# Gated linear attention's three input projections as high and low parts, with modulation strips 2 to 5 taken chunk by chunk

## What is computed

```python
mod = c_act @ mod_w[l] + mod_b[l]
sh1, sc1, g1, sh2, sc2, g2 = jnp.split(mod, 6, axis=-1)
h = modulate(x, norm_g[l, 0], sh1, sc1)
# gla_mixer(h, ...)
proj = h @ w_in
q, k, v, og, gl = jnp.split(proj, [H * dk, 2 * H * dk, 2 * H * dk + H * dv, 2 * H * dk + 2 * H * dv], axis=-1)
log_a = jax.nn.log_sigmoid((gl @ w_g2 + b_g2).astype(jnp.float32)) / GLA_GATE_TAU
...
o = rmsnorm(o, norm_g) * jax.nn.silu(og.reshape(bsz, s_len, H, dv).astype(jnp.float32))
return (o.reshape(bsz, s_len, H * dv) @ w_out).astype(h.dtype)
# back in the block
x = x + (g1[:, None, :] * y).astype(x.dtype)
h = modulate(x, norm_g[l, 1], sh2, sc2)
y = peer(h, ...)          # product-key lookup over 16384 experts
x = x + (g2[:, None, :] * y).astype(x.dtype)
```

## Time and profile before

| | |
|---|---|
| median of 3 runs | 2735.82 us (2732.2 to 2742.73) |
| the profiled execution | 2745.86 us, its span 2744.2 us |
| PE busy | 2617.0 us (95%) |
| DVE busy | 2089.5 us (76%) |
| ACT busy | 1185.9 us (43%) |
| POOL busy | 459.1 us (17%) |
| HBM traffic | 195 GB/s over the span |

### The profile page before, as it was taken

How to read it: one execution, slowest core, us unless ns; L and a number is a source line. 1 busy time by engine, 2 the same in 40 slices (tenths; PEclk the granted TensorE clock), 3 DMA queues, 4 the chain that set the end, 5 groups by cost and what they waited for, 6 DMA issues and landing times.

```text
span 2744.2 us, 49260 instructions
## 1 busy us (share of the span) xinstructions
PE 2617.0 (95%) x17458; PEld 2261.5 (82%) x17458; DVE 2089.5 (76%) x3558; ACT 1185.9 (43%) x1726; POOL 459.1 (17%) x365
## 2 busy tenths in 40 slices
PE   5999999999999998899999999999999899988998
PEld 4569999888877887889998888778888699857996
DVE  6455997888899767857978888997777777646764
ACT  1235444554434445444444454434445454423443
POOL 2001995000000000006990000000011000010000
PEclk8999999999999999899999999999999999998999
DMA  8634555555467876344555555567877456763454
GB/s 341 217 119 149 175 183 178 167 164 164 167 215 227 281 258 229 136 162 161 177 178 169 166 167 166 196 225 250 277 264 264 162 174 217 253 252 101 147 183 146
DMA packets 147627, 536.91 MB, mean 196 GB/s; under 512 B 16784, under 2 KB 17168, under 8 KB 147232
## 3 DMA queue, kind: packets, MB, share of 16 engines
q1 hardware_dynamic: 115088, 417.08, 45.3%
q0 software_dynamic: 31104, 113.26, 12.0%
q10 hardware_dynamic: 1296, 4.72, 0.4%
HBM read 531.85 MB, written 3.15 MB: 195 GB/s over the span
## 4 chain that ended last, share of the span: by engine, by line
PE 79%; DVE 9%; issue 4%; POOL 3%; DMA 2%; ACT 1%; DVEq 0%; SPq 0%; POOLq 0%; ACTq 0%
PE ps L1847 19%; PE ps L1428 9%; PE ps L2557 6%; PE ps L1404 6%; PE ps L699 6%; PE ps L1432 4%; PE ps L2539 4%; PE ps L1356 4%; PE ps L1408 3%; POOL split_lo L1479 3%; PE ps L658 3%; PE ps L1805 3%; PE ps L2543 2%; PE ps L360 2%; DVE split_lo L1491 2%
## 5 line engine op out<-in xcount | busy, mean ns | idle before, releaser
L1466 ACT ACTIVATE split_hi<-ring 128x1024 fp32r<-128x1024 f32 x740 | 779.9, 1056 | 753.8 <-PE ps L1408 200.2
L1491 DVE TENSOR_TENSOR split_lo<-ring,split_hi 128x1024 fp32r<-128x1024 f32 x552 | 673.1, 1220 | 226.2 <-ACT split_hi L1466 226.0
L1479 POOL TENSOR_TENSOR split_lo<-ring,split_hi 128x1024 fp32r<-128x1024 f32 x128 | 341.1, 2681 | 152.4 <-ACT split_hi L1466 152.1
L1463 ACT ACTIVATE gate_hi<-gate 128x256 fp32r x256 | 106.9, 418 | 441.9 <-PE ps L1847 441.9
L1847 PE MATMUL ps<-split_hi,gate_hi 128*128 128x512 f32 x1024 | 284.1, 398 | 0.0
L1847 PE MATMUL ps<-split_hi,gate_lo 128*128 128x512 f32 x1024 | 276.5, 391 | 3.6 <-DVE gate_lo L1489 3.6
L1847 PE MATMUL ps<-split_lo,gate_hi 128*128 128x512 f32 x1024 | 276.8, 391 | 0.0
L1404 PE MATMUL ps<-h_parts,split_hi 128*128 128x256 f32 x2048 | 266.8, 283 | 0.0
L1428 PE MATMUL ps<-h_parts,split_hi 128*128 128x512 f32 x1024 | 261.2, 397 | 0.0
L1404 PEld LDWEIGHTS ps<-h_parts,split_hi 128*128 128x128 f32 x2048 | 254.9, 192 | 0.0
L377 POOL DMA_DIRECT2D mod_w<-in_mod x96 | 50.8, 529 | 1139.0 <-ACT gate L1532 418.4
(11 more groups left out here) (386 smaller groups left out, 4053.2 us busy)
## 6 DMA issues: line engine op xcount, KB each, us to landing
ring<-in_stream SPq DMA_DIRECT2D x782, 512.0 KB, 4.3
mod_w<-in_mod POOLq DMA_DIRECT2D x96, 512.0 KB, 4.8
small<-in_mod POOLq DMA_DIRECT2D x80, 512.0 KB, 5.9
gate<-in_mod POOLq DMA_DIRECT2D x32, 512.0 KB, 10.5
gate<-in_mod ACTq DMA_DIRECT2D x8, 512.0 KB, 11.6
gate<-in_mod SPq DMA_DIRECT2D x8, 512.0 KB, 10.3
x_kept<-x POOLq DMA_DIRECT2D x4, 512.0 KB, 2.9
gate<-x_kept POOLq DMA_DIRECT2D x4, 512.0 KB, 9.9
```

Of the source, the lines that this page charges most:

```text
L1466: nc.scalar.activation(split_hi[:, e, :], ring[:, slot, e * D:(e + 1) * D], ACT.Copy).then_inc(hi_made, 1)
L1479: nc.gpsimd.tensor_tensor(split_lo[:, e, :], ring[:, slot, e * D:(e + 1) * D], split_hi[:, e, :].bitcast(F32), ALU.subtract).then_inc(lo_m ...
L1491: nc.vector.tensor_tensor(split_lo[:, e, :], ring[:, (START[name] + j) % RING, e * D:(e + 1) * D], split_hi[:, e, :].bitcast(F32), ALU.sub ...
```

## The change

The three projections move into `SPLIT`. `gl` and `z` go ahead of them on PE. ACT makes `gla_hi` from the normed input `hT` in four pairs of chunks and DVE the remainder `gla_lo`. The 24 tiles' high parts are placed between ACT's steps of the gates, the 24 remainders between DVE's, and the chunks of strips 2 to 5 singly between the remainders: strips 2 and 3 under `gla_qk`, `gla_v` and `gla_og`, strip 4 under `gla_out`, strip 5 under `peer_q0`. The rotary tables go behind `peer_q0` (DVE) and behind peer's first half (ACT). Two buffers are moved (`peer_qT`, the accumulators), which adds no instruction.

```diff
-SPLIT = ["gla_out", "kv", ...
+SPLIT = ["gla_qk", "gla_v", "gla_og", "gla_out", "kv", ...
...
+        def first_chunks_vector(v, first, last):
+
+            for n in range(first, last):
+                first_chunk_vector(v, 2 + n // DC, n % DC)
...
         def gla_tensor(t):
-            gemm_T(t, "gla_qk", "gla_qk", 8, DC, hT, lambda c: [f"n1.T{c}"])
             for mark in free[4]:
                 t.wait_ge(*when(mark))
             for c in range(DC):
+                t.wait_ge(*when(f"n1.T{c}"))
                 ins = nc.tensor.matmul(ps[0:16, 4, 0:SEQ], gla_wgl[:, c, :], hT[:, c, :], start=(c == 0), stop=(c == DC - 1))
             ins.then_inc(tensor_steps, t.step("gl.full"))
             gemm_z(t)
-            gemm_M(t, "gla_v", "gla_v", DC, 2, D, hT, lambda c: [], bank=0)
-            first_mod_tensor(t, (2, 3), 7)
+            split_gemm_T(t, "gla_qk", "gla_qk", 8, gla_hi, gla_lo, source="n1")
+            tile_gemm_M(t, "gla_v", "gla_v", 4, gla_hi, gla_lo, lambda c: f"n1.hi{c}", lambda c: f"n1.lo{c}", range(4))
...
-            gemm_M(t, "gla_og", "gla_og", DC, 2, D, hT, lambda c: [], bank=0)
-            first_mod_tensor(t, (4, 5), 7)
+            tile_gemm_M(t, "gla_og", "gla_og", 4, gla_hi, gla_lo, lambda c: f"n1.hi{c}", lambda c: f"n1.lo{c}", range(4))
+            first_mod_tensor(t, (2, 3), 7)
...
             out_gemm_tensor(t, "gla_out", "gla.on", gla_y)
+            first_mod_tensor(t, (4,), 0)
...
         def gla_scalar(a):
+            splits_scalar(a, "gla_qk", 0, 2)
+            for b in range(DC // 2):
+                a.wait_ge(*when(f"n1.T{2 * b + 1}"))
+                nc.scalar.activation(gla_hi[:, 2 * b:2 * b + 2, :].rearrange("p a b -> p (a b)"),
+                                     hT[:, 2 * b:2 * b + 2, :].rearrange("p a b -> p (a b)"), ACT.Copy) \
...
             turned_lo_vector(v, "gla.on", yT_lo, gla_y, bank=4)
-            less_splits_vector(v, "gla_out", 2, 8)
+            first_chunks_vector(v, 16, 18)
+            for n in range(18, 24):
+                less_splits_vector(v, "gla_out", n - 16, n - 15)
+                first_chunks_vector(v, n, n + 1)
...
             peer_turn_tensor(t, l)
+            if l == 0:
+                first_mod_tensor(t, (5,), 6)
...
-            less_splits_vector(v, f"peer_q{l}", 1, 2 * PEER_H)
+            for b in range(1, 2 * PEER_H):
+                less_splits_vector(v, f"peer_q{l}", b, b + 1)
+                if l == 0 and 4 <= b < 12:
+                    first_chunks_vector(v, b + 20, b + 21)
+            if l == 0:
+                trig_vector(v)
...
         def peer_out_scalar(a, l):
+            if l == 0:
+                trig_scalar(a)
             table_ahead_scalar(a, ACT.Sqrt)
...
             first_mod_vector(v, (1,))
+            less_splits_vector(v, "gla_qk", 0, 2)
             first_mod_store(v, (0, 1), 4)
             v.wait_ge(vector_steps, v.n)
             norm_rest_vector(v, "n1", col("norm1", 0), MOD1[0] + SC1, MOD1[0] + SH1)
-            trig_vector(v)
-            first_mod_vector(v, (2, 3))
             gla_vector(v)
```

More of the change, by code:

```diff
@@ L70 @@
     N_SLABS += _n
-SPLIT = ["gla_out", "kv", "swa_q", "swa_out", "ml_qk", "ml_v", "ml_o", "ml_out", "mla_out", "peer_q0", "u0", "v0", "peer_q1", "u1", "v1", "ffn1_0", "ffn2_0", "ffn1_1", "ffn2_1"]
+SPLIT = ["gla_qk", "gla_v", "gla_og", "gla_out", "kv", "swa_q", "swa_out", "ml_qk", "ml_v", "ml_o", "ml_out", "mla_out", "peer_q0", "u0", "v0", "peer_q1", "u1", "v1", "ffn1_0", "ffn2_0", "ffn1_1", "ffn2_1"]
 PLAIN = []
@@ L1169, in gla_scalar, with out @@
         def gla_scalar(a):
-            for g in range(4):
+            splits_scalar(a, "gla_qk", 0, 2)
[3 more added lines that the diff above has]
+                                     hT[:, 2 * b:2 * b + 2, :].rearrange("p a b -> p (a b)"), ACT.Copy) \
+                    .then_inc(scalar_steps, a.step(f"n1.hi{2 * b}"))
+                new_marks[f"n1.hi{2 * b + 1}"] = ("A", a.n)
+            a.wait_ge(*when("gl.full"))
+            nc.scalar.activation(glT[0:16, :], ps[0:16, 4, 0:SEQ], ACT.Copy).then_inc(scalar_steps, a.step("glT"))
+            def out(g):
                 a.wait_ge(*when(f"gla_qk.full{g}"))
@@ L1189, in gla_scalar @@
                 .then_inc(scalar_steps, a.step("gla.e_dec"))
+            splits_scalar(a, "gla_v", 3, 8)
+            splits_scalar(a, "gla_og", 0, 2)
             for g in range(4):
@@ L1218, in gla_vector @@
         def gla_vector(v):
+            for b in range(DC // 2):
+                v.wait_ge(*when(f"n1.hi{2 * b}"))
+                pair = slice(2 * b, 2 * b + 2)
+                nc.vector.tensor_tensor(gla_lo[:, pair, :].rearrange("p a b -> p (a b)"),
+                                        hT[:, pair, :].rearrange("p a b -> p (a b)"),
+                                        gla_hi[:, pair, :].bitcast(F32).rearrange("p a b -> p (a b)"), ALU.subtract) \
+                    .then_inc(vector_steps, v.step(f"n1.lo{2 * b}"))
+                new_marks[f"n1.lo{2 * b + 1}"] = ("V", v.n)
             for h in range(H_GLA):
@@ L1270, in gla_vector @@
                     .then_inc(vector_steps, v.step(f"gla.masked{i}"))
[L1271 to L1272 removed]
+            first_chunks_vector(v, 8, 10)
+            for n in range(10, 16):
+                less_splits_vector(v, "gla_og", n - 8, n - 7)
+                first_chunks_vector(v, n, n + 1)
+            first_mod_store(v, (2, 3), 7)
             for n in range(NCH - 1):
```

111 lines of the change are left out of this document (74 added, 37 removed).

## The result

| | before | changed |
|---|---|---|
| median of the timed runs, us | 2735.15 (2731.53 to 2743.62, 8 runs) | 2710.39 (2703.31 to 2719.16, 8 runs) |
| profiled execution, span, us | 2744.2 | 2706.8 |
| changed / before | | 0.9912, 95% interval 0.9894 to 0.993 |

The kernel became 24.8 us faster; the interval makes that 19 to 29 us. Two more measurements of the same pair gave 0.9924 (0.99 to 0.9948) and 0.9911 (0.9891 to 0.9931).

The account below looks back on a forecast made before the run. PE's products and its waits for weight slabs were taken to bound the stage: 36.6 us saved less 11.9 lost is 24.7, less 4.0 for moved work is 20.7, so 2735.82 becomes 2715; 8-in-10 range 2703 to 2727.

Parts of the forecast that it names:

- the rival with the early clock: Stage start: PE's clock is up by 45 us whatever runs; saves 8.2 more at most, 2707; chance 0.18.
- Products: The three projections on PE: 78.8 us without waits become 66.6, saving 12.2.
- The start: Before the projections: store waits 1.0; `gl` and `z` at half clock lose 5.5, `gla_qk`'s beginning 2.7.
- Hand-overs: Between ACT, DVE and PE in the three projections: 1.0 us of waits in all, upper bound 8.
- (a): Under `gla_out`: strip 4's eight chunks, one behind each remainder, delay the residual by 0.9 us.
- (b): Behind `gla_out`'s last product: strip 4's PE sum, 1.7 us, costs nothing while DVE makes the residual.
- (c): Under `peer_q0`: strip 5's chunks fit DVE's 1.65 us gaps and cost nothing; without that cover 10.2.
- (e): Rotary tables on DVE, 4.85 us, go into its 8.51 us wait for the first scores: nothing.
- (d): Between two tiles of `u0`: strip 5's sum on PE loses 1.8 us, half of 3.46.
- (f): Rotary tables' ACT step, moved to where peer's second half begins: between 0 and 1.7 us, taken as 1.3.
- Starved hand-overs: Projections: DVE's full list and chunks waiting for DMA hold back remainders; 8 us of waits, 2724; chance 0.18.
- Costly single chunks: Projections: each single chunk delays the next remainder and PE's third pass by its length; 2746 at full length; chance 0.04.

Follow-up runs that it names:

- og_plain: Changed kernel with `gla_og` plain fp32 again, whole slabs, strip 3's chunks in a row; median 2723.35 us, ratio 0.9948.
- og_four: Changed kernel with `gla_og` making high part by high part twice, four passes per tile; its products took 30.03 us, span 2709.7.
- late_sum: Changed kernel with PE making strip 0's sum only when strip 1's is due, so it idles longer; `gl` took 6.08 us.
- after_third: Changed kernel unedited, measured and traced a third time; median 2711.25 us (6 runs), ratio 0.9911.
- pairs: Changed kernel with the last six chunks of strip 3 two by two behind two remainders each; `gla_og` took 22.56 us.
- before_again: Kernel before, unedited, profiled once more; 2738.7 us, span 2736.5.
- before_busy: Kernel before plus 11 and 3 unread identity products behind strip 0's and strip 1's sums; strips stored at 150.55 us, span 2730.9.
- x_first: Changed kernel with strip 5's loads behind the copy of `x` on POOL; residual to first peer scores 59.5 us, 61.8 in the changed kernel.
- four: Changed kernel with four chunks of strip 3 in a row behind two remainders under `gla_og`; `gla_og` 23.6 us, span 2703.7.
- bunched: Changed kernel with the eight chunks of strip 2 in a row on DVE, and strip 3's likewise; median 2728.0 us, ratio 0.9978.

## Why the prediction was right, and where it was not

The forecast of 2715 (20.7 us saved) was met by 2710.4 (24.8 saved). The mechanism is the stated one, fewer passes on PE and no waits for slabs. That the number came this near is in part luck: the shares of the two were wrong and cancelled, the start was charged far too much, and the traces' lead of 28.4 us is 7.7 over the forecast; the rival with the early clock, 2707, lay as near to the result as the stated case. Two of the prediction's own signs of being wrong came true, a clock of 1.0 at 45 and peer longer by 5. By its steps:

- **What bounds it: right that PE's products and the slab's return set the stage, wrong in the shares.** "Between the pieces of a projection stand two weight DMAs ... PE loses 10.2 and 10.7 us there" is the misreading. A DMA's piece in the chain is not idle time of PE. PE was busy for 6.9 us of each of these stretches with the slab that it still had, and idle for 3.3 and 3.9: 7.2, not 20.9.
- **Products: under-sized by the same amount.** The 6.9 us pieces were missing from "78.8". PE was busy for 33.5 + 59.3 = 92.8 us before and for 22.05 + 22.35 + 22.57 = 67.0 after: 25.8 saved, not 12.2. Together with the waits it is 33.0 against 33.1 predicted. The two errors cancel, because both came from cutting the same stretch in a wrong place. Not all of the 25.8 is passes: the kernel before ran stretches of these products at 0.50 (39.7 to 45, 60 to about 65, 82.5 to 86), the changed kernel's first trace none. Four thirds of 67.0 is 89.3, so by this estimate some 3.5 of the 25.8 is the clock. og_plain (6.8 and 3.2 for one projection) and og_four show the right cut. The tile times from the earlier trace rows were good: 66.6 predicted in all, though `gla_qk` came 1.0 under its 23.0 and the other two together 1.3 over their 43.6.
  The Trainium skill (FP8 and Floating Point Precision, TensorE Precision Notes) has fp32 take four passes. The traces agree: 30.03 us for four passes, 29.4 for the plain form, 22.57 for three. On the true base of 92.8 its three quarters are 69.6, 2.6 above what was measured, since the 92.8 hold some half-clock time. I had set the rule aside because it did not fit my 78.8; that misfit was the sign that the base was wrong.
- **The start: the step that failed, 9.2 us charged.** "I take it that these narrow products do not bring the clock up" is refuted by late_sum and after_third: the clock rose to 1.00 under `gl`. In two of the three traces of the changed kernel it had not fallen at all. Nor does the half clock double `gl`: it took 6.08 us in late_sum, most of it at 0.50, and 6.41, 6.55 and 6.42 in og_plain, og_four and pairs, all at 1.00. The changed kernel's one cold start cost 0.6 (after_third), not 8.2.
  My evidence, 0.50 at 82.5, was a real dip, but one that comes behind `gl` and `z`, not under them. before_again has it too (0.50 from 83 to 86), before_busy has not; of the eleven traces with `gl` first, four have it (og_plain, og_four, pairs, late_sum), each time with `gl` at 6.08 us or more, and it costs `gla_qk` 1.5. None of the changed kernel's own three has it. What brings it, and why `gl` takes 5.1 to 5.8 us in some executions and over 6 in others, is open.
  What is real in this step in the first trace is 1.6: from the start of `gl` to the end of `z` takes 7.6 in place of 6.0, as `gl` now comes first and its weight loads wait for the normed input's chunks from DVE (4.7 us in four waits). The 1.0 us for the store's delay did come: the strip sum ended at 37.55, and the store began behind the remainder of 37.30, at 38.44. It does not show in the first product's 39.60, because the sum began 0.5 earlier in this execution, at 33.97, and because `gl`'s first product needs one chunk of the normed input (0.55 in the chain) where `gla_qk`'s came behind two (1.01).
- **Slow start of `gla_og`:** 22.57, 0.8 over 8 x 2.72, for the 1.7 counted. **Hand-overs:** 1.5 to 1.6 for the 1.0 counted, but not where I looked. None is a wait for a remainder; they are ACT's copies out of PSUM ahead of `gla_v` (1.07) and `gla_og` (0.46).
- **Stage:** predicted 24.7 net, measured 33.5. Of the 8.8, 7.6 are the start's (9.2 - 1.6); the rest are small terms of either sign.
- **Moved out:** predicted 4.0, measured 5.1, the 33.5 less the 28.4 at `v0`. (a) Strip 4's last chunk costs nothing: the lead at the residual is still 33.5, for the 0.9 expected. (b), (c), (e) cost nothing, as said. (d) Strip 5's sum cost 30.9 - 29.1 = 1.8, as said. (f) The table step on ACT cost 0.7 for 1.3. What I had only in a rival, strip 5's loads against the copy of `x`, cost some 2.3 for the 2 put there, 1.3 by the copy and 1.0 by the clock behind it; x_first takes both away.
- **The sum** is then 33.5 - 5.1 = 28.4, which is the lead in the traces from `v0` on. The timed runs have 24.8, 23.8 and 22.3 between their medians, with intervals from 14 to 30. That traces show some 4 us more than runs is not explained; half-clock stretches differ from execution to execution by as much, and the dip behind `gl`, with the longer `gl` ahead of it some 3 us, is in none of the changed kernel's three traces.
- **Rivals.** The early clock came true as far as it went, though not for its reason alone. Starved hand-overs did not: DVE has a tile in hand, and from 47 to 123 us no remainder, high part or chunk waited for a DMA in the groups by line, though the DMA share was 0.95 under `gla_og`. The Trainium skill's rule (DMA: Bandwidth & Descriptors, Queues, rings and completion order) has an engine take turns between its queues. The traces agree: in x_first, beside strip 5's loads, two weight halves landed in 7.0 us at the median where the changed kernel's took 3.6 without them. It is just no loss here, as nothing waited for those halves. The earlier trace rows did not speak against the rule, as I had it: landing is counted from issue, and a strip load waits behind others of POOL's own queue (in x_first the eight land 5.2 to 12.5 us after issue, the later the slower). The copy of `x` is on that queue too, so its wait behind strip 5's loads is no case of turns between queues. Costly single chunks: refuted by pairs and four. What that rival feared is real only for long rows, as bunched shows.

## What to carry to other kernels

A DMA's duration in the chain of waits is not the time that PE lost: ask the group's idle column, or count the instructions of the pieces against the group's. When a known ratio of passes does not fit a sum of durations, recount the sum before setting the ratio aside.
Filling work goes between two remainders as long as it is shorter than what the buffers hold in reserve: here one tile of PE, some 2.8 us, beside the engine's own gap; two chunks were free, four cost 0.8, eight cost 6, and a stall of 6 costs half as much again, by the clock that falls in it.
A low clock in a single trace says little about its place: the same kernel had it at the start in one trace of three. Take a second trace before charging it.

## What the runs showed of the hardware

- The same 16 one-column products of strip 0's sum took either 1.8 to 2.2 us or 3.41 us, in the same kernel too: 1.84 in one of its three traces, 3.41 in the other two. Where they were short, PE idled 4.5 to 5.0 us before the next sum, and the clock was 0.50 from about 31 on; where they were long, it idled 3.3 and stayed at 1.00. Nine of the ten traces that begin as the changed kernel does have the long sum and the full clock, both of the kernel before the short one. Why the same products take two durations is open.
- An extra pass costs the same as the others to 0.1 us (7.46 for 8 tiles), and the plain fp32 form costs four of them.
- The copy of `x` waited for in the chain took 4.3 to 4.8 us in the changed kernel's three traces, with strip 5's eight loads ahead of it on POOL's queue, 3.03 in both kernels that had them behind it, and 2.88 in the kernel before.
